# Spreading a projection's matrix products between the small products at the head of each delta-rule turn

## The reference

```python
proj = h @ w_in
(sc_b, sc_c, sc_x, dn_q, dn_k, dn_v, dn_z, dn_a, dn_b, gate_sc, gate_dn) = split_cols(proj, IN_SIZES)
br_sc = (sc_b * causal_dwconv(sc_c * sc_x, sc_conv_w)) @ w_sc_out
...
G = jnp.cumsum(gc, axis=-1)
decay = jnp.where(incl, jnp.exp(jnp.where(incl, diff, 0.0)), 0.0)
L = jnp.einsum('bhnid,bhnjd->bhnij', kb, kc) * jnp.where(strict, decay, 0.0)
sol = lax.linalg.triangular_solve(eye + L, rhs, left_side=True, lower=True, unit_diagonal=True)
...
v_new = u_n - jnp.einsum('bhck,bhkv->bhcv', w_n, S)
o = jnp.einsum('bhck,bhkv->bhcv', qg_n, S) + jnp.einsum('bhij,bhjv->bhiv', a_n, v_new)
S = S * gl_n[..., None, None] + jnp.einsum('bhck,bhcv->bhkv', kd_n, v_new)
```

## Time and profile before

| | |
|---|---|
| runs | 1857.79, 1857.22, 1857.72 us |
| median | 1857.72 us |
| span of the profiled execution | 1856.8 us |
| between span and median | 0.9 us |
| TensorE busy | 1768.2 us, 95% of the span |
| VectorE, GpSimd, ScalarE busy | 1307.3, 764.5, 742.8 us |

### The profile page before, as it was taken

One profiled execution on the slowest core, in us unless ns is written; L12 is line 12 of the kernel. 1 busy time (PEld: TensorE's weight loads), 2 busy tenths in 40 slices (PEclk: granted clock), 3 DMA queues, 4 the chain that ended last, 5 costly groups with the idle time before them and its releaser, 6 DMA issues. The chain is left out here.

```text
span 1856.8 us, 31058 instructions
## 1 busy us (share of the span) xinstructions
PE 1768.2 (95%) x11485; PEld 1564.7 (84%) x11485; DVE 1307.3 (70%) x2777; ACT 742.8 (40%) x1227; POOL 764.5 (41%) x449
## 2 busy tenths in 40 slices
PE   3999999999998989999999999879999999999998
PEld 2666888878877889999999999879998888888887
DVE  5993454553224679878869999756787888777777
ACT  4332332242234233333337767633333333333334
POOL 2333232344442448777753333122454443332330
PEclk9998999999999999999999999989999999999999
DMA  9661101022322249888868999978899999889883
GB/s 356 217 233 71 36 16 34 25 91 91 102 79 103 91 141 314 282 292 292 286 235 281 341 311 331 319 264 285 287 317 337 370 370 359 326 320 328 316 325 145
DMA packets 179267, 432.64 MB, mean 233 GB/s; under 512 B 15816, under 2 KB 91720, under 8 KB 179040
## 3 DMA queue, kind: packets, MB, share of 16 engines
q1 hardware_dynamic: 125088, 273.71, 42.5%
q0 software_dynamic: 36864, 134.23, 20.3%
q10 hardware_dynamic: 17216, 23.36, 3.4%
HBM read 383.54 MB, written 47.71 MB: 232 GB/s over the span
## 5 line engine op out<-in xcount | busy, mean ns | idle before, releaser
L201 POOL DMA_INDIRECT own_rows<-in_peer_v_dram,own_row x128 | 212.3, 1659 | 330.8 <-DVE y_own L2094 312.7
L1988 PE MATMUL banks<-v_hi,coef_lo 128*128 128x512 f32 x756 | 294.6, 390 | 0.0
L1988 PE MATMUL banks<-v_lo,coef_hi 128*128 128x512 f32 x756 | 294.5, 390 | 0.0
L1988 PE MATMUL banks<-v_hi,coef_hi 128*128 128x512 f32 x756 | 294.1, 389 | 0.1
L201 POOL DMA_INDIRECT own_rows<-in_u_rows_dram,own_row x128 | 160.6, 1255 | 233.1 <-DVE own_rows L1733 178.8
L2079 DVE TENSOR_TENSOR v_lo<-weight_ring,v_hi 128x1024 fp32r<-128x1024 f32 x128 | 156.5, 1222 | 24.7 <-ACT v_hi L2027 22.7
L1988 PEld LDWEIGHTS banks<-v_hi,coef_hi 128*128 128x128 f32 x756 | 142.0, 188 | 29.5 <-issue 0.5
L1988 PEld LDWEIGHTS banks<-v_hi,coef_lo 128*128 128x128 f32 x756 | 141.9, 188 | 29.5
L1988 PEld LDWEIGHTS banks<-v_lo,coef_hi 128*128 128x128 f32 x756 | 141.9, 188 | 28.9
L2094 DVE SCALAR_TENSOR_TENSOR y_own<-own_rows,own_coef,y_own 128x1024 f32<-128x1024 f32 x128 | 163.8, 1279 | 1.9 <-DVE y_own L2094 0.5
L1397 PE MATMUL banks<-h_hi,wring_hi 128*128 128x384 f32 (+2 forms) x448 | 155.2, 347 | 4.0 <-ACT gelu_early L1479 2.9
(11 more groups left out here) (393 smaller groups left out, 4346.1 us busy)
## 6 DMA issues: line engine op xcount, KB each, us to landing
weight_ring<-in_peer_v_dram SPq DMA_DIRECT2D x128, 512.0 KB, 5.4
weight_ring<-in_peer_u_dram SPq DMA_DIRECT2D x68, 512.0 KB, 4.5
ada<-in_w_ada_dram SPq DMA_DIRECT2D x48, 512.0 KB, 5.7
gate_scratch<-gate_block SPq DMA_DIRECT2D x48, 512.0 KB, 7.0
gate_tiles<-gate_scratch SPq DMA_DIRECT2D x32, 768.0 KB, 6.9
gelu_scratch<-gelu_early ACTq DMA_DIRECT2D x104, 192.0 KB
gelu<-gelu_scratch SPq DMA_DIRECT2D x104, 192.0 KB, 5.6
u_early<-in_peer_u_dram SPq DMA_DIRECT2D x36, 512.0 KB, 7.1
```

Source lines behind the costliest of these rows:

```text
L201: pool.indirect_dma_start(own_rows[:, n % R], None, tables[n // NS], bass.IndirectOffsetOnAxis(ap=own_row[:, n % NS:n % NS + 1], axis=0)). ...
L1988: last = nc.tensor.matmul(y_bank(t, half)[:], w[:, j, t * P:(t + 1) * P], x[:, j, c], start=(first and n == 0), stop=False)
```

## The change

In each turn TensorE no longer runs the 24 products of tile `3*tt+1` in one piece behind the transposes. Six stand behind the decay rows, three behind `betaT`, three behind `GT`, three behind `kX`, nine behind `vX`. For that the tile's parts must be ready at the head's start: ScalarE splits tile `3*tt+4` right behind tile `3*tt+3`, and GpSimd makes its low part at the end of the turn and no longer behind the next turn's copy.

```diff
@@ ScalarE, a turn's second half
                     split(3 * tt + 3)
+                    split(3 * tt + 4)
                     act.wait_ge(*E.after("wT", tt))
...
                     nc.scalar.activation(ost[:, 1, :], ost[:, 0, :], ACT.Sqrt, bias=eps[:], scale=1.0 / DK).then_inc(*A.step("ostd"))
-                    split(3 * tt + 4)
@@ GpSimd
                     nc.gpsimd.tensor_copy(qkv[:], qkvT[:, :, slice(tt * P, tt * P + P)]).then_inc(*Q.step("tile"))
-                    if tt:
-                        rest(3 * tt + 1)
                     rest(3 * tt + 2)
...
                     rest(3 * tt + 3)
-                rest(3 * TT + 1)
+                    rest(3 * tt + 4)
@@ TensorE, a turn's head
                         last.then_inc(*E.step(f"grow{g}"))
+                    sc_product(3 * tt + 1, slice(0, 2))
                     pe.wait_ge(*V.after("oT", tt, 1))
                     group("betaT", 2, lambda j: (sel_pair[:, j, :], rows[:, 1, tok]))
+                    sc_product(3 * tt + 1, slice(2, 3))
                     group("GT", 3, lambda j: (sel_pair[:, j, :], rows[:, 0, tok]))
+                    sc_product(3 * tt + 1, slice(3, 4))
                     pe.wait_ge(*Q.after("tile", tt))
                     group("kX", 4, lambda j: (qkv[:, HJ + j, :], None), transpose=True)
+                    sc_product(3 * tt + 1, slice(4, 5))
                     group("vX", 5, lambda j: (qkv[:, 2 * HJ + j, :], None), transpose=True)
-                    sc_product(3 * tt + 1)
+                    sc_product(3 * tt + 1, slice(5, KT))
                     pe.wait_ge(*V.after("kb", tt))
```

## The result

The changed kernel takes 1863.12 us (median of 22 runs, 1857.06 to 1869.1); the kernel before, beside it on the same chip, 1857.22 us (22 runs, 1854.13 to 1859.42). The ratio is 1.0033, 95% interval 1.0024 to 1.0043: slower by 0.33%, 5.9 us, where 1856.0 us was forecast.

What follows compares the result with a forecast made beforehand. TensorE was taken to bound the delta stage, its heads slowed by a low clock. Four heads gain 3.4 us, one clock fall costs 1.7: -1.7 from 1857.7 gives 1856.0 us, range 1852.5 to 1864.5.

Steps and rivals of the forecast that it cites:

- The head: Turn's start, first decay row to first kk: 12.00 us before, 11.15 with clock kept, gaining 0.85 us (0.16 to 1.08).
- The lost clock: In each turn's head, 3.41 us at 0.50 clock cost 1.6 us (1.38 to 1.70), regained if the clock stays up.
- The added changes of kind: In each turn's head, more switches between small and large products or transposes cost 0.75 us (0.62 to 1.22).
- A fall in one head of four: Likeliest case, chance 0.36: clock falls in one or two heads; one costs 1.7 us, giving 1856.0 us.
- The banks in turn: New head cycles PSUM banks 6, 2, 6, 3, 6, 4, 6, 5, 6; a skill rule warns of clock toggling, doubted here.
- ScalarE's split: Moved ahead of wT, it adds 1.05 us within 2.74 us of idle: hidden with 1.7 us left.
- SyncE's loads: Issued some 16 us sooner in the delta stage, whose DMA share is 0.09: no effect.
- GpSimd's low part: Moved to 258.8 to 261.1, beside VectorE's state_decayed; 0.57 us idle before v_new covers stretching: cost 0, bound 0.5 a turn.
- The rival that ended slower: Clock falls early in the head, before betaT and GT end, for 6.82 us: +10.2 us, 1867.9 us; chance 0.26.
- its signs: If head lengths miss the span's change, look to wT, VectorE beside GpSimd, or low stretches in later stages; no size given.

Runs made afterwards that it cites:

- the fill without pieces: Kernel before, heads in one piece, six of tile 3*tt+3's products put into state-update gaps in turns 0 to 2, that tile split earlier: 1854.34 us, ratio 0.9986.
- three pieces: Changed kernel plus six products of tile 3*tt+3 in state-update waits (turns 0 to 2), head's 24 products as 6, 6 and 12: 1852.82 us, ratio 0.9978.
- two pieces: Changed kernel plus six products of tile 3*tt+3 in state-update waits (turns 0 to 2), head's 24 products as 6 and 18: 1851.83 us, ratio 0.9974.

## Why the prediction was wrong

*The head* was right in each term. The lost clock was put at 1.6 us a head: 11.98 to 10.43 in the fill without pieces is 1.55. The added changes of kind were put at 0.75: 11.12 - 10.43 is 0.69. The head was put at 11.15 us with the clock kept and takes 11.11 to 11.14. A fall in one head of four was thought likeliest; the profiled run has none, five variants with the same head have one each (12.67 to 12.71 us; 12.8 was forecast), five of 24 in all. The banks in turn did no harm in the profiled run: the four heads ran at 1.00. The Trainium skill, "TensorE: Matmul & The Clock Gate", section "A second HAM failure mode: psum-queue depth-cycling", tells of a kernel whose clock went up and down with such cycling; this trace doesn't bear it out.

*ScalarE's split* was right as to `wT`: the pair of splits takes 1.99 us from 203.53, and 1.79 us of idle remain ahead of `wT` (1.7 forecast). Overlooked was that in the last turn the late split had kept the low part off `state_decayed`, as the run with the split alone shows. *SyncE's loads* come sooner, a DMA share of 0.19 to 0.28 in the updates of turns 0 to 2 in place of 0.13 or 0.14, and cost nothing: the run with 0.28 has the 12.15 us of before.

*GpSimd's low part* is the step that failed: "Cost 0, bound 0.5 a turn". `state_decayed` lost 1.43 us in each of three turns and 1.13 in the last. The bound came from L934, 0.95 in place of 0.42, read as if beside GpSimd an operation took about twice as long. But the prediction had the times for a better one: low part until 261.1, `state_decayed` from 259.50. An operation that must wait for GpSimd's end takes 1.6 + 0.42 = 2.0 us, and 1.85 was measured. Past the 0.57 us of idle that makes `v_new` 0.79 late and TensorE's wait 0.75. The row that the bound came from says the same, if GpSimd's row beside it is read:
```profile
289.25 1.20 POOL L737 TENSOR_TENSOR CT<-LT,cst 128x256 f32<-128x256 f32 x1
```
GpSimd ends at 289.25 + 1.20 = 290.45, and L934 at 289.78 + 0.95 = 290.73, 0.28 behind it. In the 17 meetings of `state_decayed` with a low part in all profiled runs it ends 0.28 or 0.29 us behind GpSimd, however long that makes it. The rule stands in the Trainium skill, "SBUF — State Buffer", section "Who interferes with whom": a VectorE operation with both inputs in SBUF contends with GpSimd's reads, and whichever comes second is fully blocked until the first is done. The trace agrees: `state_decayed` ends 0.28 us behind GpSimd in all four turns, while `scT`, with one operand in the banks, takes 0.68 both beside GpSimd and, in the run with VectorE made late, without it.

*The size* of the loss then came from a step that wasn't there. A wait of 0.8 us in four turns is about 3 us, and the heads give back 3.6: alone that would have been no change. But the updates are 64x64 products with idle between them, and with that wait added the clock fell there for 10.24 us, in two turns of the profiled run fully and in one for 3.41 us. A full fall costs 3.73 us (16.67 against 12.94). Over all profiled runs, the clock fell in 10 of the 17 updates with the added wait (nine times for 10.24 us, once for 3.41), in none of 23 without it, and in none of 16 in which large products stood in the waits. The rival that ended slower had the clock fall in the head; it fell in a stage that the prediction had left at nothing, for lack of asking which stretch had the least work to spare once `v_new` was late. Both VectorE beside GpSimd and low stretches elsewhere stood among its signs, but with no price. Holding the low part back (5 us better), taking it forward (5 us better), and putting the wait in without it (as slow as the change, with one fall in its trace) show this cause; that GpSimd's place alone, without the head, costs even more shows that the pieces didn't bring it. That 1863.12 us lies between the stated 1852.5 and 1864.5 is luck: that end of the range stood for a fall in the head.

What stays open: with the low part out of the way the head's gain of 2.2 us in the profiled run doesn't reach the total, as what follows the delta stage took 1.9 us more. Over the profiled runs that part tends to be longer where more of it stands at 1.2 GHz: 1480.18 us with 32.9 us at that clock (three pieces), 1481.98 with 39.7 (before), 1483.87 with 42.8 (low part held back), 1486.38 with 45.7 (two pieces). Why it stands so long in one run and less in another isn't shown. By the medians the pieces are worth 0.2 us here (1858.46 against 1858.65), with intervals of 2 us to either side.

## What to carry to other kernels

Before moving GpSimd work on SBUF tiles, write down its start and end and look for every VectorE operation in that stretch that has both operands in SBUF: count it as ending behind GpSimd, not as twice as long, and follow what it delays. A short wait of TensorE (0.5 to 0.8 us here) in a stretch of small products with idle time in it can cost several times its length through TensorE's clock; the same products of the next tile that were to be done anyway were the cheaper of the two covers tried. And where work is broken into pieces to keep the clock, try the fewest pieces first: one break of the run of 8-row products did here what four did.

## What was not expected of the hardware

A VectorE multiplication of 0.42 us took 1.55 to 2.47 us when it began inside a GpSimd subtraction of about 2.35 us. Once the clock fell in the state updates it stayed at 1.2 GHz for 10.24 us in nine cases of ten, three times the 3.41 of the old heads, with TensorE busy throughout.
